# Expert blocks of a mixture of experts: gather and store only rows that hold a token, outputs scattered into the order of assignments

## What is computed

```
g_idx = argmax(xt @ w_rg + b_rg)                  # one of 4 groups
top_v, top_i = top_k(e_logits of that group, 2)   # 2 of its 8 experts
gate = p_g * softmax(top_v)
# 2048 assignments, sorted by expert, in padded blocks of 128 rows, one expert each
buf_tok = zeros(P).at[dest_sorted].set(tok_flat[order])
hb = silu(xb @ w1[e]) * (xb @ w3[e]);  out = hb @ w2[e]
y_assign = out_buf[dest].reshape(N, 2, D)
y = einsum('nk,nkd->nd', gate, y_assign)
```

## Time and profile before

| | |
|---|---|
| median of 3 runs | 3003.52 us (3000.16 to 3004.29) |
| the profiled execution, its own time | 2999.86 us |
| its span, first to last instruction | 2998.0 us |
| TensorE busy | 87% of the span |
| VectorE, ScalarE, GpSimd busy | 40%, 39%, 35% |
| experts, from the table to the next block of code | 2272 to 2948 us |
| combine | 2948 to 2998 us |

### The profile page before, as it was taken

How to read it: one execution, slowest core, us unless ns; L and a number is a source line. 1 busy time by engine, 2 the same in 40 slices (tenths; PEclk the granted TensorE clock), 3 DMA queues, 4 the chain that set the end, 5 groups by cost and what they waited for, 6 DMA issues and landing times. The chain is left out here.

```text
span 2998.0 us, 31014 instructions
## 1 busy us (share of the span) xinstructions
PE 2611.4 (87%) x12104; PEld 2115.2 (71%) x12104; DVE 1207.2 (40%) x1640; ACT 1176.7 (39%) x1699; POOL 1045.6 (35%) x619
## 2 busy tenths in 40 slices
PE   6999978889699999899988695988966999999991
PEld 5888856667587878688867584865865777777770
DVE  4530137742312202223446404014126666666664
ACT  3212227751331221222324403324034777777762
POOL 3212203321321221413204512543102776666762
PEclk9999989999799999999989896999957999999995
DMA  4433145512410121322144324361264999999976
GB/s 152 146 116 104 37 113 130 134 47 92 161 57 28 64 106 43 105 83 94 58 145 134 114 85 154 113 253 42 92 247 174 376 374 384 376 373 375 375 300 245
DMA packets 173024, 494.54 MB, mean 165 GB/s; under 512 B 13936, under 2 KB 81552, under 8 KB 160208
## 3 DMA queue, kind: packets, MB, share of 16 engines
q1 hardware_dynamic: 120160, 391.01, 36.7%
q0 software_dynamic: 14944, 52.78, 4.8%
q10 hardware_dynamic: 37776, 48.77, 4.5%
HBM read 397.62 MB, written 94.90 MB: 164 GB/s over the span
## 5 line engine op out<-in xcount | busy, mean ns | idle before, releaser
L213 POOL TENSOR_TENSOR p_w_lo<-p_w_raw,p_w_hi 128x512 fp32r<-128x512 f32 (+1 forms) x248 | 320.3, 1327 | 825.9 <-ACT p_w_hi L233 824.0
L2427 ACT ACTIVATE ex_w_hi<-ex_w 128x2048 fp32r<-128x2048 f32 x198 | 378.7, 1916 | 168.5 <-DMA ex_w<-w 101.6
L2487 DVE TENSOR_TENSOR ex_w_lo<-ex_w,ex_w_hi 128x2048 fp32r<-128x2048 f32 x132 | 349.2, 2683 | 195.2 <-ACT ex_w_hi L2427 195.2
L2311 POOL TENSOR_TENSOR ex_w_lo<-ex_w,ex_w_hi 128x2048 fp32r<-128x2048 f32 x66 | 340.9, 5187 | 203.2 <-ACT ex_w_hi L2427 203.2
L233 ACT ACTIVATE p_w_hi<-p_w_raw 128x512 fp32r<-128x512 f32 (+1 forms) x224 | 127.1, 610 | 183.2 <-DMA p_w_raw<-w_in 52.5
L392 PE MATMUL o_ps<-o_w_hi,o_m_hi 128*128 128x512 f32 x384 | 153.0, 398 | 18.8 <-POOL o_m_lo L1013 18.8
L392 PE MATMUL sgu_ps<-p_w_hi,h2T_hi 128*128 128x512 f32 x384 | 150.9, 393 | 2.6 <-PEq L273 2.6
L393 PE MATMUL o_ps<-o_w_lo,o_m_hi 128*128 128x512 f32 x384 | 152.5, 397 | 0.0
L394 PE MATMUL o_ps<-o_w_hi,o_m_lo 128*128 128x512 f32 x384 | 152.1, 396 | 0.0
L393 PE MATMUL sgu_ps<-p_w_lo,h2T_hi 128*128 128x512 f32 x384 | 150.2, 391 | 0.0
L394 PE MATMUL sgu_ps<-p_w_hi,h2T_lo 128*128 128x512 f32 x384 | 150.1, 391 | 0.0
(11 more groups left out here) (386 smaller groups left out, 6402.2 us busy)
## 6 DMA issues: line engine op xcount, KB each, us to landing
ex_w<-w SPq DMA_DIRECT2D x99, 2048.0 KB, 10.9
p_w_raw<-w_in SPq DMA_DIRECT2D x42, 1024.0 KB, 5.2
y_slots<-ex_y ACTq DMA_DIRECT2D x33, 512.0 KB, 12.2
y_slots<-xp_zero POOLq DMA_DIRECT2D x32, 512.0 KB, 16.6
att_k<-k_columns SPq DMA_DIRECT2D x48, 256.0 KB, 7.6
x_rows<-o_y SPq DMA_DIRECT2D x24, 512.0 KB, 2.8
n_x<-x_rows SPq DMA_DIRECT2D x24, 512.0 KB, 5.0
o_w_raw<-w_out SPq DMA_DIRECT2D x8, 1024.0 KB, 10.0
```

The costliest lines, as they stand in the source:

```text
L213: emit(self.lo[:, n % self.R, 0:w], self.half(n // (KC // 2), w)[:, n % (KC // 2), :], self.hi[:, n % self.R, 0:w].bitcast(F32), ALU.subtr ...
L2311: nc.gpsimd.tensor_tensor(w_lo[:, n % RING, :], raw_half(n), w_hi[:, n % RING, :].bitcast(F32), ALU.subtract).then_inc(down_lo, 1)
L2427: nc.scalar.activation(w_hi[:, n % RING, :], raw_half(n), ACT.Copy).then_inc(hi_done, 1)
L2487: nc.vector.tensor_tensor(w_lo[:, n % RING, :], raw_half(n), w_hi[:, n % RING, :].bitcast(F32), ALU.subtract).then_inc(up_lo, 1)
```

## The change

1. `y_slots` (6144 rows by block and place) becomes `y_rows` (2048 rows: row k*1024 + t is the output for token t's k-th expert). The clearing in memory_projections is gone: tile, memset, 32 stores and the wait.
2. route writes two tables, `slot_token` and `slot_row`; an empty place gets an index past the end. GpSimd clears both buffers of gathered rows, `xg`, once. `dest` is gone.
3. In experts the gather has a bounds check that leaves out rows with such an index, and y is no longer stored by ACT but scattered by an indirect DMA from GpSimd, also with a bounds check. The scatter of block b-2 stands in GpSimd's order between the `w_lo` of w2a and that of w2b of block b-1; the last two follow at the end.
4. In combine the two sets of y are read by plain loads, one from SP (between those of x), the other from ACT.

```diff
@@ memory_projections
-                nc.gpsimd.memset(zero[:, :], 0.0).then_inc(zero_ready, 1)
-                pool.wait_ge(zero_ready, 1)
-                if y_slots is not None:
-                    for b in range(2 * S // P, NBLK):
-                        pool.dma_start(y_slots[b * P:(b + 1) * P, :], zero[:, :]).then_inc(cleared, 16)
-                    pool.wait_ge(cleared, 16 * NE)
@@ route
+            @block.gpsimd
+            def _(pool):
+                nc.gpsimd.memset(xg[:, :, :], 0.0)
...
-                step(V.tensor_copy(dest[:, :, :], dest_f[:, :, :]))
...
-                    ins = V.tensor_tensor(d2[:, k * NT:(k + 1) * NT, :], d2[:, k * NT:(k + 1) * NT, :],
-                                          c.const("tokid").unsqueeze(2).to_broadcast([P, NT, NBLK]), ALU.mult)
+                    half = d2[:, k * NT:(k + 1) * NT, :]
+                    ins = V.scalar_tensor_tensor(half, c.const("tokid").unsqueeze(2).to_broadcast([P, NT, NBLK]),
+                                                 float(k * S + 1), half, ALU.add, ALU.mult)
...
-                V.memset(slot_token[:, NBLK:], 0)
-                step(V.tensor_copy(slot_token[:, 0:NBLK], pt[:, 0:NBLK]))
+                step(V.tensor_scalar(d2[:, 0, :], pt[:, 0:NBLK], 0.5, float(NOWHERE), ALU.is_lt, ALU.mult))
+                step(V.scalar_tensor_tensor(d2[:, 1, :], pt[:, 0:NBLK], -1.0, d2[:, 0, :], ALU.add, ALU.add))
+                V.tensor_copy(slot_row[:, :], d2[:, 1, :])
+                step(V.tensor_scalar(d2[:, 2, :], d2[:, 1, :], float(S), -float(S), ALU.is_ge, ALU.mult))
+                step(V.tensor_tensor(slot_token[:, :], d2[:, 1, :], d2[:, 2, :], ALU.add))
@@ experts, GpSimd
                     nc.gpsimd.indirect_dma_start(xg[:, b % 2, :], None, xn,
-                                                 bass.IndirectOffsetOnAxis(slot_token[:, b:b + 1].bitcast(U32), 0)
-                                                 ).then_inc(x_in[b % 2], 16)
+                                                 bass.IndirectOffsetOnAxis(slot_token[:, b:b + 1].bitcast(U32), 0),
+                                                 bounds_check=S - 1, oob_is_err=False).then_inc(x_in[b % 2], 16)
+
+                def scatter(b):
+                    pool.wait_ge(y_ready, b + 1)
+                    nc.gpsimd.indirect_dma_start(y_rows, bass.IndirectOffsetOnAxis(slot_row[:, b:b + 1].bitcast(U32), 0),
+                                                 y[:, b % 2, :], None, bounds_check=2 * S - 1, oob_is_err=False
+                                                 ).then_inc(y_out[b % 2], 16)
...
+                    if m == "w1" and half == 1 and b >= 2:
+                        scatter(b - 2)
+                scatter(NB - 2)
+                scatter(NB - 1)
@@ experts, ScalarE
-                    act.wait_ge(y_ready, b + 1)
-                    act.dma_start(y_b[b], y[:, b % 2, :]).then_inc(y_out[b % 2], 16)
@@ combine
                     sp.dma_start(x[:, t, :], x_t[t]).then_inc(x_in[t], 16)
+                    sp.dma_start(y[:, t, 0, :], y_rows[t * P:(t + 1) * P, :]).then_inc(y_in[t], 16)
...
-                        nc.gpsimd.indirect_dma_start(y[:, t, k, :], None, y_slots,
-                                                     bass.IndirectOffsetOnAxis(dest[:, k, t:t + 1].bitcast(U32), 0)
-                                                     ).then_inc(y_in[t], 16)
...
+                for t in range(NT):
+                    act.dma_start(y[:, t, 1, :], y_rows[S + t * P:S + (t + 1) * P, :]).then_inc(y_in[t], 16)
```

More of the change, by code:

```diff
@@ L46 @@
 NBLK = NE + NEXTRA
+NOWHERE = 8 * S
 CONST_COLS = dict(ident=P, ones=P, causal=P, before=P, iota=P, tokid=NT, blk=NBLK, sel=MH * P, iota32=NT * NE,
@@ L1849, in memory_weights, with memory_projections @@
     return Weights(c, stack, "p3", sources, groups, side="right")
-def memory_projections(c, weights, xT, mnT, qT, kT, v, y_slots=None):
+def memory_projections(c, weights, xT, mnT, qT, kT, v):
     nc = c.nc
@@ L2006, in _, with cross_attention @@
                         keep_out((i - 7) // 4 * 2 + 1)
-def cross_attention(c, x2, x3, y_slots=None):
+def cross_attention(c, x2, x3):
     nc, io = c.nc, c.io
@@ L2020, in cross_attention @@
             v = s.enter_context(nc.sbuf_tensor("v3", [P, NMEM // P, D], F32))
-            memory_projections(c, weights, hT, mnT, qT, kT, v, y_slots)
+            memory_projections(c, weights, hT, mnT, qT, kT, v)
         weights = out_weights(c, s, "o3", io["w_xo_2"])
@@ L2034, in load_router, with route @@
     sp.dma_start(bias[:, NG:], io["b_re_2"].partition_broadcast(P)).then_inc(w_in, 16)
-def route(c, pl, bias, gates, dest, slot_token, extra_expert, n_rest):
+def route(c, pl, bias, gates, slot_token, slot_row, extra_expert, n_rest, xg):
     nc = c.nc
@@ L2208, in load, with experts @@
         sp.dma_start(self.w2s[:, b % 2, :], self.w2[at].rearrange("e p n -> (e p) n")).then_inc(self.w2_in[b % 2], 16)
-def experts(c, weights, xn, y_slots, slot_token, n_rest):
+def experts(c, weights, xn, y_rows, slot_token, slot_row, n_rest, xg):
     nc = c.nc
     KF, HALF, RING, NB = FF // P, KC // 2 * FF, 4, NE + 1
-    y_b = y_slots.rearrange("(b p) d -> b p d", p=P)
     def steps():
@@ L2251, in experts @@
         w_hi, w_lo = sb("w_hi", [P, RING, HALF], F32R), sb("w_lo", [P, RING, HALF], F32R)
-        idx, xg = sb("idx", [P, 1], I32), sb("x", [P, 2, D])
+        idx = sb("idx", [P, 2], I32)
         xT_hi, xT_lo = sb("xT_hi", [P, D], F32R), sb("xT_lo", [P, D], F32R)
@@ L2321, in _ @@
                         gather(b + 2)
+                    if m == "w1" and half == 1 and b >= 2:
+                        scatter(b - 2)
+                scatter(NB - 2)
+                scatter(NB - 1)
                 def regather(i):
                     pool.wait_ge(r_free, i + 1)
-                    nc.gpsimd.tensor_copy(idx[:, :], slot_token[:, bass.ds(i + NB, 1)]).then_inc(r_idx, 1)
+                    nc.gpsimd.tensor_copy(idx[:, 0:1], slot_token[:, bass.ds(i + NB, 1)])
+                    nc.gpsimd.tensor_copy(idx[:, 1:2], slot_row[:, bass.ds(i + NB, 1)]).then_inc(r_idx, 1)
                     pool.wait_ge(r_idx, i + 1)
@@ L2328, in regather @@
                     nc.gpsimd.indirect_dma_start(xg[:, 0, :], None, xn,
-                                                 bass.IndirectOffsetOnAxis(idx[:, :].bitcast(U32), 0)
-                                                 ).then_inc(r_x_in, 16)
+                                                 bass.IndirectOffsetOnAxis(idx[:, 0:1].bitcast(U32), 0),
+                                                 bounds_check=S - 1, oob_is_err=False).then_inc(r_x_in, 16)
+                    pool.wait_ge(r_y_ready, i + 1)
+                    pool.sem_inc(r_gathers, 1)
+                    nc.gpsimd.indirect_dma_start(y_rows, bass.IndirectOffsetOnAxis(idx[:, 1:2].bitcast(U32), 0),
+                                                 y[:, 0, :], None, bounds_check=2 * S - 1, oob_is_err=False
+                                                 ).then_inc(r_y_out, 16)
                 over_rest(pool, regather)
@@ L2472, in block_of_rest @@
                     nc.scalar.activation(y[:, 0, :], p_y[:, :], ACT.Copy).then_inc(r_y_ready, 1)
-                    act.wait_ge(r_y_ready, i + 1)
-                    act.dma_start(y_b[bass.ds(i + NB, 1)].rearrange("e p n -> (e p) n"), y[:, 0, :]).then_inc(r_y_out, 16)
                     act.wait_ge(r_y_out, 16 * i + 16)
@@ L2526, in _, with combine @@
                 over_rest(dve, block_of_rest)
-def combine(c, x3, y_slots, dest, gates, out):
+def combine(c, x3, y_rows, gates, out):
     nc, io = c.nc, c.io
@@ L2595, in _, with mixture @@
                 norm(NT - 1)
-def mixture(c, x3, xn, y_slots, out):
+def mixture(c, x3, xn, y_rows, out):
     nc, io = c.nc, c.io
@@ L2601, in mixture @@
         gates = s.enter_context(nc.sbuf_tensor("gates", [P, 2, NT], F32))
-        dest = s.enter_context(nc.sbuf_tensor("dest", [P, 2, NT], I32))
-        slot_token = s.enter_context(nc.sbuf_tensor("slot_token", [P, NBLK + 1], I32))
+        slot_token = s.enter_context(nc.sbuf_tensor("slot_token", [P, NBLK], I32))
+        slot_row = s.enter_context(nc.sbuf_tensor("slot_row", [P, NBLK], I32))
         extra_expert = s.enter_context(nc.sbuf_tensor("extra_expert", [P, NEXTRA], I32))
@@ L2607, in mixture @@
             weights = ExpertWeights(c, s1, extra_expert)
+            xg = s1.enter_context(nc.sbuf_tensor("ex_x", [P, 2, D], F32))
             with ExitStack() as s2:
@@ L2615, in mixture @@
                                     router=(wr, bias, logits), experts=weights)
-                route(c, logits, bias, gates, dest, slot_token, extra_expert, n_rest)
-            experts(c, weights, xn, y_slots, slot_token, n_rest)
-        combine(c, x3, y_slots, dest, gates, out)
+                route(c, logits, bias, gates, slot_token, slot_row, extra_expert, n_rest, xg)
+            experts(c, weights, xn, y_rows, slot_token, slot_row, n_rest, xg)
```

(7 more changed lines are left out.)

2 lines of the change are left out of this document (removed).

## The result

The changed kernel takes 3030.9 us (median of 4 runs, 3027.4 to 3031.8), the kernel before 3003.9 beside it on the same chip: ratio 1.009, 95% interval 1.0073 to 1.0108, so 27.0 us more. The forecast was 3037 with 2996 to 3064 and 0.80 on slower. The profiled executions have spans of 2998.0 and 3025.5, 27.5 apart.

What follows compares the result with a forecast made beforehand. GpSimd's rest of w2b, not transfers, was taken to pace experts; terms 40 - 6 + 0.6 + 2 - 2.5 = +34 us on 3003.5 gave 3037 us, range 2996 to 3064, slower 0.80.

Steps and rivals of the forecast that it cites:

- experts: Expert blocks: the scatter between GpSimd's two pieces adds 1.3 us in each of 31 blocks, +40 us.
- its end: End of experts: GpSimd issues the last y and starts its empty loop only then, +2 us, bounds 0 and 5.
- memory_projections: End of memory_projections: removing the clearing stores closes the gap to the next block, -6 us, bounds -4 and -8.
- route: In route: five small steps replace the last one and a `dest` step goes, +0.6 us, bounds 0 and 2.5.
- combine: In combine: plain loads bring the first tile 2 to 4 us earlier, the last 2.5; -2.5 us, bounds 0 and -7.
- What bounds it: In experts: GpSimd's rest of w2b paces the loads; the loop of 19.55 us a block has no transfer in it.
- The scatter's price: In experts: 0.94 to 1.03 us as for gathers, plus 0.30, so 1.3 us; bounds 0.4 and 3.3.
- The 0.30 to the next instruction: On GpSimd in experts: time between an indirect DMA and the next instruction, 0.30 us added to each scatter.
- The order of VectorE and GpSimd: In experts: VectorE goes first during the scatter, costing 1.4 to 2.2 us a block; mixed with cheaper blocks, 0.85 to 1.8.
- Bytes: In experts: moving 0.54 of 7.34 MB less a block, 7.4%, is worth nothing in the present loop.
- The rate of 381 GB/s: In combine: at the clearing's 381 GB/s, 25 tiles of 13.1 MB take 34 us either way.
- the bound of -8: End of memory_projections: lower bound of the -6 us term; the shorter idle may save the clock some.

Runs made afterwards that it cites:

- experiment 4: The kernel before with a 128x1024 memset between GpSimd's two pieces in 31 blocks; 3029.1 us, ratio 1.0095.
- experiment 11: experiment 4 with a memset twice as long (128x2048) between GpSimd's two pieces; 3055.5 us, ratio 1.0177.
- experiment 12: The kernel before with y of the 33 blocks scattered, all 128 rows, by GpSimd between its two pieces instead of ACT's store; 3041.3 us, ratio 1.0134.
- experiment 1: The changed kernel with the scatter issued right behind the gather, no longer between GpSimd's two pieces; 2993.4 us, ratio 0.9969.
- experiment 5: The changed kernel with the scatter issued ahead of GpSimd's first piece instead of between its two pieces; 2992.6 us, ratio 0.9963.
- experiment 6: experiment 2 with the rest of w2b moved from GpSimd to VectorE, all rows still moved; 2950.0 us, ratio 0.9824.
- experiment 7: experiment 1 with the rest of w2b moved from GpSimd to VectorE, half the row traffic; 2948.7 us, ratio 0.9823.
- experiment 10: The changed kernel with the rest of w2b moved from GpSimd to VectorE, the scatter left in its place; 2949.6 us, ratio 0.9825.
- experiment 3: experiment 2 with bounds-checked gathers, the table steps and the memset of `xg`; ACT still stores all rows of y; 2993.8 us, ratio 0.9973.
- experiment 2: The kernel before, clearing only blocks 33 to 47, with 15 stores instead of 32; 2992.3 us, ratio 0.9969.
- experiment 8: experiment 2 with six GpSimd memsets behind ACT's last instruction of memory_projections; 3003.7 us, ratio 1.0004.
- experiment 9: experiment 2 with combine reading y by plain loads from SP and ACT instead of 16 gathers; 2991.7 us, ratio 0.9963.

## Why the prediction was right, point by point

The sum of the profiled executions, by marks: experts up to TensorE's last product +35.4 (40 predicted), its end +1.05 (+2), memory_projections -6.2 (-6), the attention stage behind it -4.0 (not in the sum), the start of project_out -1.3 (not in the sum), route +0.85 (+0.6), combine -0.8 (-2.5), and +2.2 ahead of all of it (0). That is +27.2 of the 27.5. The experts' term is 28 periods of +1.27, 35.6; what lies ahead of them and behind them comes to -0.2. The forecast is 7 us too high by 4.6 in experts, 4.0 of the clock and 1.0 at the end of experts, less 1.7 in combine; the +2.2 and the -1.3 are not the change's, as shown below.

**What bounds it.** Right, and shown from three sides: the loop through GpSimd's rest of w2b gets longer by what stands between the pieces (experiments 4, 11, 12), doesn't when the same instruction stands elsewhere (1, 5), and the period falls to TensorE's own work when the rest is taken off GpSimd (6, 7, 10). Transfers, at a share of 0.93, bounded nothing.

**The scatter's price.** 0.94 to 1.03 taken from the gathers, 1.00 to 1.01 measured. The 0.30 to the next instruction was too much: the first piece's end to the scatter is 0.14, its end to the second piece 0.04, and the pair with the scatter grew by 1.19. Steady blocks cost 1.22, with the exceptions below 1.27 on average. That the average meets the 1.3 so closely is in part luck: the exceptions make up for a gap that was put too long.

**The order of VectorE and GpSimd.** Here a step was off, though its result stood. I expected VectorE, asking for its piece while GpSimd scatters, to go first. In 5 of 30 blocks it does, when it asks up to about 0.2 us after the scatter's start; then its piece takes 2.3 us. Asking 0.36 us or later it stands still until GpSimd's second piece ends, 7.34 us in the block shown, although that piece hasn't started when it asks. Of the five, the gathers show the length of four: 21.9 to 22.1 us, 2.4 to 2.6 over the period of before where I had 1.4 to 2.2, and the block after one of them 18.6 to 20.1, so the mix moves the mean only from 20.77 to 20.82. What decides between the two stays open: no experiment took it apart.

**Bytes.** Priced at nothing, right: 19.56 with half the row traffic (experiment 1), 19.56 with the gathers' half (3), 20.82 with all rows and with half (12 and the change; the 5 us behind the last gather in experiment 12 stay open). Even with TensorE as the bound they are worth at most 0.12 us a block. The rate of 381 GB/s that the prediction took for combine was too low as well: the loads there run at 415 (experiments 6 and 7).

**memory_projections.** The gap was -6.2 as said. What the sum left out is the clock: I had it only in the bound of -8 ("may save the clock some"). The attention stage is 4.0 us shorter, shown by experiments 2 and 8 to be the price of the idle. This is the largest missed term, mis-sized at 0 where it was 4. project_out's start, 1.3 us shorter in the changed kernel, isn't the clearing's: from SP's first `o_x` to its first store of `o_y` it takes 19.15 us in the kernel before and 17.86 in the changed one, but 17.66 in experiment 4, which has the idle, and 19.13 in experiment 1, which hasn't.

**route, the end, combine.** +0.85 for four steps more is right in kind. The end costs 1.05 where I had 2: the last scatter starts 0.78 us after ACT's last copy of y where the store started 0.03 after it, and from there to the next block it is 12.97 for 12.66 us, so GpSimd's empty loop over the rest blocks was hardly late. Combine gained a third of what I gave it; experiment 9 gives 0.9 alone by its arithmetic and 0.56 by its end. Both versions move 17.3 MB at 346 GB/s over combine, so only the first tile's start could gain, and it gained 0.9 us, not 2 to 4. The Trainium skill, DMA: Bandwidth & Descriptors, section "Issuing engine by pattern", calls DMAs from SP or ACT generally the faster ones; in combine, plain loads from them in place of GpSimd's gathers are so by 0.9 us.

**The 2.2 us ahead.** A stretch near 1565 us, whose code is the same in both, ran at a granted clock of 0.71 in the profiled execution of before and 0.50 in that of the changed kernel. It isn't the change's: experiment 11, which up to there is the kernel before, has 0.50 as well, and over all the kernels here ACT's last instruction of memory_projections starts between 2001.6 and 2007.1 us.

The profiled execution of before was 3.7 us below its median, which fits. Put on the medians, the forecast's difference of 34 stands against 27.0.

## What to carry to other kernels

Before an instruction goes onto an engine, ask what that engine does behind it and who waits there: the same scatter cost 1.2 us a block between two pieces, and nothing at 2.0 or 2.9 us beside or behind them. A saving of bytes is worth what the loop that sets the period lets through, and here even a DMA share of 0.93 didn't mean that transfers set it. When a helper engine paces the loop, the larger gain is to take work off it: one piece moved from GpSimd (4.5 us) to VectorE (2.2 us) made this kernel 2949 us, 1.8% faster than before, with either way of storing y; 0.3% of it is the clearing's (experiment 2), the rest the moved piece's.

## What the runs showed of the hardware

- An indirect DMA's time on GpSimd goes by what VectorE does, not by rows: 1.00 us for 128 rows and for the half-filled blocks; up to 3.1 when it starts while VectorE is in a `tensor_tensor` of 128x2048, as it then ends 0.8 to 0.9 after that piece. Beside combine's `scalar_tensor_tensor` of 128x1024 it stays at 0.94. The Trainium skill, SBUF — State Buffer, section "Who interferes with whom", infers that tensor_tensor leaves descriptor writing alone. Experiments 5 and 10 (1.98 and 2.88 us) show that the instruction as a whole isn't left alone. But the last 0.88 us of each run beside VectorE's next piece, and in the five blocks of the changed kernel where VectorE's piece starts with the scatter or up to 0.2 us behind it, the scatter takes its 1.00 us. So it is the start that waits, and no run here shows that writing descriptors is what is held.
- A memset between GpSimd's pieces delays the second by its own length (0.96 and 1.81 us). VectorE, asking during a scatter, can be shut out by a GpSimd piece that has not begun (7.34 us for a piece of 2.3).
- The DMA engines moved 402 GB/s at a share of 0.99 (experiment 6) and 415 in the combine of the kernel before, where 368 at 0.93 had looked like a ceiling.
- A TensorE idle of 7.1 to 8.5 us costs about 4 us more behind it, by a lower granted clock in the first 6 us (0.50 to 0.60); behind one of 0.91 us the clock is 1.00.
